# Forgetting attention in a two-layer encoder: another order of the TensorE work inside a step, and one VectorE wait narrowed

## The chip, the cores and the metric

One NeuronCore of a Trainium2 chip runs the whole kernel. The metric is the device time of one execution in microseconds. Three runs of the kernel before gave 1349.3, 1349.78 and 1350.14 us; the median is 1349.78 us.

## What is computed

The kernel computes two layers of an encoder over 512 tokens with 1024 features. Layer 0 mixes a gated recurrence with differential attention; layer 1 is forgetting attention. Each layer ends with an output projection, a layer norm, a SwiGLU block and another layer norm. The change touches the forgetting attention alone:

```python
def _fox_attention(q, k, v, c):          # 16 heads of width 64, 512 tokens
    ...
        s = jnp.einsum('bhqd,bhkd->bhqk', qb, k) * scale + (cb[..., :, None] - c[..., None, :])
        q_pos = start + jnp.arange(Q_BLOCK)
        mask = k_pos[None, :] <= q_pos[:, None]
        p = jax.nn.softmax(jnp.where(mask, s, MASK_VALUE), axis=-1)
        return jnp.einsum('bhqk,bhkd->bhqd', p, v)

def _odd_mixer(x, w_in, w_out, b_f, qn_g, kn_g):
    proj = x @ w_in
    q, k, v, g, f_logit = jnp.split(proj, [D_MODEL, 2 * D_MODEL, 3 * D_MODEL, 4 * D_MODEL], axis=-1)
    ...
    o = _fox_attention(qh, kh, vh, c).reshape(Bsz, S, D_MODEL)
    o = o * jax.nn.sigmoid(g.astype(F32))
    return o.astype(x.dtype) @ w_out
```

The per-row term c_t falls out of the softmax; what is added to the scores is -c_s, and a mask of -1e30 above the diagonal.

## The kernel before, in words

**Weight products.** Every projection is made of three fp32r products (`products`, lines 560 to 563: lines L561, L562, L563 of the profile) that split both operands into a high and a low part. ScalarE makes the high part of the weights (L1328), GpSimd the low part (L1281). A "piece" is a quarter of a 2048-column weight chunk against one tile of tokens: 12 matmuls with 512 moving columns, or 24 with 256.

**The work of the attention.** The 16 heads form 8 pairs, and each pair has 4 blocks of 128 queries: 32 units. Unit u belongs to pair u // 4 and to query block i = u % 4, and has (i + 1) * 128 keys. A unit passes through these stages:

- scores (`pair_scores`, line 1121): for each head of the pair one product of queries and keys (L1132; 64 rows of the array are used, head 0 the lower half, head 1 the upper), one product that adds -c_s (L1137; bf16, 48 rows in the same halves), and one product that adds the mask to the last 128 columns (L1140; bf16, all 128 rows). The mask product closes the bank. The two banks are two of the banks 5, 6 and 7.
- VectorE takes the row maximum (L2047, or L2050 and L2051), ScalarE the exponential and its row sum (L1644, semaphore fexp), VectorE multiplies by the reciprocal (L2058, L2061; semaphore fnorm).
- turn (`turn_pair`, line 1143): TensorE transposes the probabilities (L1148; all 128 rows and columns), head 0 into bank 3, head 1 into bank 4. It first waits for fnorm of its unit and for each bank's last reader.
- ScalarE copies bank 3 out (`prob_copy`, L1572), VectorE copies bank 4 out (L2070).
- values (`pair_values`, line 1152): products of v and the turned probabilities (L1167; 64 columns of the array are used, head 0 the lower half, head 1 the upper) into bank 2. When the four blocks of a pair are done, VectorE copies bank 2 out (L2089, or L2009).

**The order.** A list written at build time, `fox_steps` (lines 391 to 400), interleaves the pieces of the remaining projections (queries and keys "h", values "v", gates "g") with the steps s = 0 to 34. Every engine walks the same list in its own program. An entry is (piece, s) or (piece, None); in some stretches one piece stands between two steps, in others two, and before steps 30 to 33 one piece of the output projection. In an entry TensorE does, in this order: the piece; at some entries the transposes of freshly normed queries and keys (`turn_heads`, L1118), which also go into bank 3 and which ScalarE copies out (L1581); then, with a step s, scores of unit s with their mask, turn of unit s - 2, values of unit s - 3.

ScalarE does, in an entry with step s: copies of the last piece's bank (L1350 and L1600), the copy of turned queries and keys (L1581), rounding of a weight chunk (L1328), then the exponential of unit s, which waits for VectorE's maximum, and behind it the copy of bank 3 of unit s - 2. VectorE does the norm work of queries and keys, then the maximum of unit s, the scaling of unit s - 1, the copy of bank 4 of unit s - 2, and then whatever reads bank 2 (unit s - 3). Pieces take banks 0 and 1 in turn; a piece that begins a new result waits until ScalarE has copied the result before last out of that bank.

The lines that matter in `open_bank` and in the two transposing functions:

```python
                if last[bank]:
                    who, count = last[bank]
                    pe.wait_ge(freed[who][bank], count)
...
                acc = open_bank(key, 3, "act")                                   # turn_heads
...
                    acc = open_bank(("fT", u, m), 3 + m, ("act", "dve")[m])      # turn_pair
```

and the end of a step in ScalarE's program:

```python
                    act.wait_ge(S["fmax"], s + 1)
...
                    act.sem_inc(S["fexp"], 1)
                if s is not None and 2 <= s < F_UNITS + 2:
                    prob_copy(s - 2)
```

Of the kernel before, what the change touches and what calls it, by code (L numbers as in the profile page):

```python
# [39 lines left out]
P = 128  # L40
D = 1024
TS = 512
NT = TS // P
# [22 lines left out]
PAIRS = FH // 2  # L66
# [76 lines left out]
def build(nc, w, out):  # L143
# [5 lines left out]
    with ExitStack() as ctx:  # L149
# [24 lines left out]
        ident_bf = place("ident_bf", [P], BF16, 2)  # L174
        fox_mask = place("fox_mask", [P], BF16, 2)
# [71 lines left out]
        psum = [banks[:, b, :] for b in range(8)]  # L247
# [66 lines left out]
        def chunk_at(stage, i=0):  # L314
            return stage_chunks[stage][i]
# [22 lines left out]
        n = 0  # L338
# [51 lines left out]
        F_UNITS = PAIRS * NT  # L390
# [133 lines left out]
        def _(pe):  # L524
# [13 lines left out]
            def close_bank(key, ins):  # L538
                ins.then_inc(bank_full[uses[key][0]], 1)
# [46 lines left out]
            def token_chunk(c, reader, src_hi, src_lo, k_base, first, final, width=512, places=None):  # L586

                stage, _, size = chunks[c]
                nk = size // width
                if c in by_piece:  # L590
                    pe.wait_ge(hi_ready, c + 1)
                else:
                    weights_in(c)
                for t in range(NT):
                    key = (stage, t) if not isinstance(final, tuple) else (*final, t)
                    if first:
                        open_bank((stage, "acc", t, c), places[t] if places else next_gemm_bank(), reader)
                        acc_bank[t] = uses[(stage, "acc", t, c)]
                    acc = psum[acc_bank[t][0]][:, 0:width]
                    for k in range(nk):  # L600
                        if c in by_piece and t == 0:
                            piece_in(c, k)
                        tok = slice(t * P, (t + 1) * P)
                        ins = products(acc, src_hi[:, k_base + k, tok], src_lo[:, k_base + k, tok],
                                       hi(c, k * width, width), lo(c, k * width, width),
                                       first and k == 0, bool(final) and k == nk - 1)
                    if final:
                        uses[key] = acc_bank[t]
                        close_bank(key, ins)
                    if t == NT - 1:  # L610
                        if final:
                            used_with_bank(c, key)
                        else:
                            used_alone(c, ins)
                    yield
# [505 lines left out]
            def pair_scores(s):  # L1121
                pair, i = s // NT, s % NT
                j, n = s // PART_UNITS, (i + 1) * P
                if s == 0:
                    pe.wait_ge(S["c_in"], 16 * 6)
                if s % PART_UNITS == 0:
                    pe.wait_ge(S["qk_done"], NT * (j + 1))
                    pe.wait_ge(S["v_done"], NT * max(1, j))
                accs = [open_bank(("fs", s, m), SCORE_BANKS[s % 3][m], "act") for m in range(2)]
                for m, acc in enumerate(accs):  # L1130
                    rows = slice(m * HD, (m + 1) * HD)
                    mm(acc[:, 0:n], qk[rows, j % 2, 0, pair % 2, i * P:(i + 1) * P], qk[rows, j % 2, 1, pair % 2, 0:n],  # L1132
                       start=True, stop=False)
                for m, acc in enumerate(accs):
                    h = 2 * pair + m
                    rows = slice(m * HD, m * HD + 3 * FH)
                    mm(acc[:, 0:n], pick[rows, h:h + 1].to_broadcast([3 * FH, P]), c_rows[rows, 0:n],  # L1137
                       start=False, stop=False)
                for m, acc in enumerate(accs):
                    close_bank(("fs", s, m), mm(acc[:, n - P:n], ident_bf[:, :], fox_mask[:, :],  # L1140
                                                start=False, stop=True))

            def turn_pair(u):
                pe.wait_ge(S["fnorm"], u + 1)
                for m in range(2):
                    acc = open_bank(("fT", u, m), 3 + m, ("act", "dve")[m])
                    for j in range(u % NT + 1):
                        ins = nc.tensor.transpose(acc[:, j * P:(j + 1) * P], p_fox[:, u % 3, m, j * P:(j + 1) * P],  # L1148
                                                  ident[:, :])
                    close_bank(("fT", u, m), ins)  # L1150

            def pair_values(u):
                pair, i = u // NT, u % NT
                pe.wait_ge(S["fpT_a"], u + 1)
                pe.wait_ge(S["fpT_b"], u + 1)
                bank = 5 if u == F_UNITS - 1 else 2
                if i == 0 or pair == PAIRS - 1:
                    open_bank(("fv", u), bank, "dve")
                else:

                    bank_count[2] += 1
                    uses[("fv", u)] = (2, bank_count[2], "dve")
                tok = slice(i * P, (i + 1) * P)
                for j in range(i + 1):
                    for m in range(2):
                        h = 2 * pair + m
                        ins = mm(psum[bank][m * HD:(m + 1) * HD, tok], v_all[:, j, h * HD:(h + 1) * HD],  # L1167
                                 pT_fox[:, u % 2, m, j * P:(j + 1) * P], start=j == 0, stop=j == i)
                close_bank(("fv", u), ins)

            first_out[1] = token_chunk(chunk_at("out1"), "dve", o_hi4, o_lo4, 0, True, False, places=(0, 1, 6, 7))
            for i, (piece, s) in enumerate(fox_steps):
                if piece and i >= len(HEAD_LEAD) - 1:
                    stage = chunks[piece[0]][0]
                    if stage not in running:
                        if stage[3] == "h":
                            running[stage] = heads_chunk(int(stage[4]), HEAD_ORDER)
                        elif stage == "foxv0":
                            running[stage] = columns(stage, "act", places=(5, 7, 6, 2))
                        elif stage[3] == "g":  # L1180
                            running[stage] = feature_chunk(piece[0], "act")
                        else:
                            running[stage] = token_chunk(piece[0], "act", xT_hi, xT_lo, 0, True, True, 256)
                    next(running[stage])
                if heads_at(i - TURN_LAG):
                    turn_heads(*heads_at(i - TURN_LAG))
                if s is None:
                    continue
                if F_UNITS - 2 <= s < F_UNITS + 2:
                    if s == F_UNITS - 2:  # L1190
                        for gen in running.values():
                            drain(gen)
                        pe.wait_ge(S["o_hi"], 4)
                        pe.wait_ge(S["o_lo"], 4)
                    next(first_out[1])
                if s < F_UNITS:
                    pair_scores(s)
                if 2 <= s < F_UNITS + 2:
                    turn_pair(s - 2)
                if s >= 3:  # L1200
                    pair_values(s - 3)
            gemm_banks[0] = 4
            fox_out()
            swiglu(1)
# [463 lines left out]
        def _(dve):  # L1668
# [349 lines left out]
            for i, (piece, s) in enumerate(fox_steps):  # L2018
# [53 lines left out]
                if s is not None and s >= 3:  # L2072
                    u = s - 3
                    pair, t = u // NT, u % NT
                    acc = full(("fv", u))
                    if pair == PAIRS - 1:
                        tok = slice(t * P, (t + 1) * P)
                        release(out_gate(pair, acc[:, tok], tok), ("fv", u))
                        dve.sem_inc(S["o_gated"], 1)
                        if t == 0:  # L2080
                            out_lo(4)
                            out_lo(5)
                            out_lo(PAIRS - 2)
                        out_lo(pair, tok, t)
                    elif t == NT - 1 and pair == PAIRS - 2:
                        release(out_gate(pair, acc[:, :]), ("fv", u))
                        dve.sem_inc(S["o_gated"], 1)
                    elif t == NT - 1:
                        release(v.tensor_copy(oT[:, pair, :], acc[:, :]), ("fv", u))  # L2089
# [64 lines left out]
```

## Time and profile before

| | before |
|---|---|
| median of three runs | 1349.78 us |
| the profiled execution | 1350.16 us |
| its span, first to last instruction | 1348.1 us |
| steps 0 to 31, from the first scores to the last values | about 712 to 943 us of the span |
| TensorE matmul (PE) busy | 1334.4 us, 99% |
| TensorE weight load (PEld) busy | 1092.7 us, 81% |
| VectorE (DVE), ScalarE (ACT), GpSimd (POOL) busy | 454.5, 480.0, 529.8 us |

A row of the timeline gives the start of a group of like instructions in us from the start of the span, the time from the first start to the last end, the engine, the line, the operation, what it writes and reads, the shapes and the count. A matmul's own length in it is a latency: the next one starts long before it ends. So the time that a group costs TensorE is read from its start to the start of the next group. Two matmuls of fp32 data stand for one product in L1132 and L1167. A bracket at the end gives idle time of the engine before the group and who ended it.

### The profile page before, as it was taken

To read this page: it belongs to the slowest core of one execution; us is meant where nothing else is said; L and a number is where in the kernel's file an instruction comes from. 1 tells how busy PE (TensorE), PEld (TensorE's weight loads), DVE (VectorE), ACT (ScalarE), POOL (GpSimd) and SP (SyncE) were. 2 spreads that over 40 slices of the span, in tenths; PEclk is the share of its full clock that TensorE was granted. 3 is DMA by queue.
4 is the path that set the end of the run, shared out by engine and by line. 5 is a ranking of instruction groups with operands and counts; after the bars stand their busy time and mean duration, and the time that the engine had idled before them with its cause. 6 is when DMAs were issued, how large, how long until landed. Compare 5 with 4: busy or idle time off the path is not lost.

```text
span 1348.1 us, 17988 instructions
## 1 busy us (share of the span) xinstructions
PE 1334.4 (99%) x6943; PEld 1092.7 (81%) x6943; DVE 454.5 (34%) x857; ACT 480.0 (36%) x759; POOL 529.8 (39%) x421
## 2 busy tenths in 40 slices
PE   9999999999999999999999999999999999999997
PEld 7888877788888888888787877677898888888886
DVE  4364446771111111011643554545621111110105
ACT  3413266533222223211365554644332222222120
POOL 4422433334444444543352332323244444435440
PEclk9999999999999999999999999999999999999999
DMA  6301121314333332323123212313133333333221
GB/s 213 123 32 63 63 94 63 95 38 119 95 94 94 95 101 90 137 94 109 47 84 94 63 33 63 95 63 95 32 110 110 94 94 94 94 109 107 107 84 63
DMA packets 141540, 119.55 MB, mean 89 GB/s; under 512 B 5808, under 2 KB 120720, under 8 KB 141456
## 3 DMA queue, kind: packets, MB, share of 16 engines
q1 hardware_dynamic: 141216, 118.10, 27.9%
q8 instruction: 56, 0.92, 0.3%
q10 hardware_dynamic: 240, 0.31, 0.1%
q14 instruction: 28, 0.23, 0.1%
HBM read 116.20 MB, written 2.10 MB: 88 GB/s over the span
## 4 chain that ended last, share of the span: by engine, by line
PE 96%; DVE 2%; issue 1%; ACT 0%; DMA 0%; POOL 0%; SPq 0%; DVEq 0%; ACTq 0%; POOLq 0%
PE banks L561 28%; PE banks L563 28%; PE banks L562 28%; PE banks L989 2%; PE banks L1132 2%; PE banks L1167 2%; PE banks L1148 1%; PE banks L674 1%; PE banks L1080 1%; PE banks L1007 1%; PE banks L1067 1%; PE banks L1140 1%; PE banks L1118 0%; DMA x_res<-in_x_dram 0%; PE banks L1094 0%
## 5 line engine op out<-in xcount | busy, mean ns | idle before, releaser
L1281 POOL TENSOR_TENSOR w_lo<-w_raw,w_hi 128x512 fp32r<-128x512 f32 x417 | 529.6, 1299 | 786.9 <-ACT w_hi L1328 523.7
L561 PE MATMUL banks<-xT_lo,w_hi 128*128 128x512 f32 (+2 forms) x1024 | 383.7, 375 | 0.9 <-DVEq L1688 0.7
L563 PE MATMUL banks<-xT_hi,w_hi 128*128 128x512 f32 (+2 forms) x1024 | 380.0, 371 | 0.0
L562 PE MATMUL banks<-xT_hi,w_lo 128*128 128x512 f32 (+2 forms) x1024 | 379.9, 371 | 0.0
L1328 ACT ACTIVATE w_hi<-w_raw 128x2048 fp32r<-128x2048 f32 (+1 forms) x106 | 198.2, 1869 | 174.5 <-PE banks L563 145.6
L561 PEld LDWEIGHTS banks<-xT_lo,w_hi 128*128 128x128 f32 (+1 forms) x1024 | 191.4, 187 | 35.7 <-issue 3.3
L563 PEld LDWEIGHTS banks<-xT_hi,w_hi 128*128 128x128 f32 (+1 forms) x1024 | 191.3, 187 | 34.0
L562 PEld LDWEIGHTS banks<-xT_hi,w_lo 128*128 128x128 f32 (+1 forms) x1024 | 191.5, 187 | 32.6
L1960 DVE TENSOR_TENSOR banks<-silu_g,banks 128x512 f32<-128x512 f32 x44 | 30.6, 696 | 402.3 <-PE banks L563 402.3
L561 PE MATMUL banks<-w_lo,xT_hi 128*128 128x512 f32 (+1 forms) x352 | 135.9, 386 | 1.6 <-ACT q_raw L1350 0.7
L561 PE MATMUL banks<-w_lo,hT_hi 128*128 128x512 f32 x352 | 137.1, 390 | 0.0
L563 PE MATMUL banks<-w_hi,hT_hi 128*128 128x512 f32 x352 | 137.0, 389 | 0.0
L562 PE MATMUL banks<-w_hi,hT_lo 128*128 128x512 f32 x352 | 136.9, 389 | 0.0
L1544 ACT ACTIVATE silu_g<-banks 128x512 f32<-128x512 f32 x44 | 26.4, 599 | 306.7 <-PE banks L563 306.6
L563 PE MATMUL banks<-w_hi,xT_hi 128*128 128x512 f32 (+1 forms) x352 | 130.6, 371 | 0.0
L562 PE MATMUL banks<-w_hi,xT_lo 128*128 128x512 f32 (+1 forms) x352 | 130.5, 371 | 0.0
L1892 DVE SCALAR_TENSOR_TENSOR x_res<-x_res,banks 128x512 f32<-128x512 f32 x32 | 22.0, 688 | 204.9 <-PE banks L563 203.8
L561 PEld LDWEIGHTS banks<-w_lo,xT_hi 128*128 128x128 f32 x352 | 66.3, 188 | 16.4 <-issue 4.0
L562 PEld LDWEIGHTS banks<-w_hi,hT_lo 128*128 128x128 f32 x352 | 66.1, 188 | 13.7
L563 PEld LDWEIGHTS banks<-w_hi,hT_hi 128*128 128x128 f32 x352 | 66.1, 188 | 13.7
L561 PEld LDWEIGHTS banks<-w_lo,hT_hi 128*128 128x128 f32 x352 | 66.1, 188 | 13.7
L563 PEld LDWEIGHTS banks<-w_hi,xT_hi 128*128 128x128 f32 x352 | 66.3, 188 | 12.0
(196 smaller groups left out, 1214.6 us busy)
## 6 DMA issues: line engine op xcount, KB each, us to landing
w_raw<-in_ffn_w_dram SPq DMA_DIRECT2D x92, 512.0 KB, 4.4
w_raw<-in_ffn_w_dram SPq DMA_DIRECT2D x20, 1024.0 KB, 4.9
w_raw<-in_even_w_in_dram SPq DMA_DIRECT2D x13, 1024.0 KB, 4.8
w_raw<-in_fox_w_in_dram SPq DMA_DIRECT2D x16, 512.0 KB, 4.4
w_raw<-in_fox_w_in_dram SPq DMA_DIRECT2D x8, 1024.0 KB, 5.6
w_raw<-in_even_w_out_dram SPq DMA_DIRECT2D x4, 1024.0 KB, 4.9
w_raw<-in_fox_w_out_dram SPq DMA_DIRECT2D x4, 1024.0 KB, 4.9
x_res<-in_x_dram SPq DMA_DIRECT2D x4, 512.0 KB, 7.1
```

The source lines that it names most:

```text
L561: mm(acc, l_hi, r_lo, start=first, stop=False)
L562: mm(acc, l_lo, r_hi, start=False, stop=False)
L563: return mm(acc, l_hi, r_hi, start=False, stop=final)
L674: ins = nc.tensor.transpose(acc[:, j * P:(j + 1) * P], src[:, t, f:f + P], ident[:, :])
L989: ins = mm(halves(acc[:, tok], z)[:, :, 1, :], k[:, tok], halves(q[:, tok], z)[:, :, 1, :], start=True, stop=True)
L1132: mm(acc[:, 0:n], qk[rows, j % 2, 0, pair % 2, i * P:(i + 1) * P], qk[rows, j % 2, 1, pair % 2, 0:n], start=True, stop=False)
L1167: ins = mm(psum[bank][m * HD:(m + 1) * HD, tok], v_all[:, j, h * HD:(h + 1) * HD], pT_fox[:, u % 2, m, j * P:(j + 1) * P], start=j == 0, s ...
L1281: ins = nc.gpsimd.tensor_tensor(w_lo[c % RING][:, a:a + n], w_raw[c % RAW][:, a:a + n], w_hi[c % RING][:, a:a + n].bitcast(F32), ALU.subtract)
L1328: chain(fn(w_hi[c % RING][:, 0:size], w_raw[c % RAW][:, 0:size], ACT.Copy), hi_ready)
L1544: release(fn(silu_buf(j), acc[:, :], ACT.Silu), (f"up{l}", j, 0))
L1892: release(stt(xs, xs, ALPHA, full(key)[:, :], ALU.mult, ALU.add), key)
L1960: release(tt(h_buf(j), silu_buf(j), acc[:, :], ALU.mult), (f"up{l}", j, 1))
```

## The change

Inside a step TensorE now does: turn of unit s - 2, scores of unit s without the mask, values, and last the masks of unit s. The values of units s - 4 and s - 3 are done together in every second step (s = 4, 6, ..., 30); steps 31 to 34 do one unit each, as before. VectorE no longer waits in every step for the values of unit s - 3; it waits in the steps in which it reads bank 2. The programs of ScalarE, GpSimd and the queues are as they were, and so is `fox_steps`.

```diff
@@ pair_scores, and the new pair_masks
                        start=False, stop=False)
-                for m, acc in enumerate(accs):
-                    close_bank(("fs", s, m), mm(acc[:, n - P:n], ident_bf[:, :], fox_mask[:, :],
+
+            def pair_masks(s):
+
+                n = (s % NT + 1) * P
+                for m, b in enumerate(SCORE_BANKS[s % 3]):
+                    close_bank(("fs", s, m), mm(psum[b][:, n - P:n], ident_bf[:, :], fox_mask[:, :],
                                                 start=False, stop=True))
@@ after pair_values
+            def values_of(s):
+
+                if s >= F_UNITS - 1:
+                    return [s - 3]
+                return [s - 4, s - 3] if s >= 4 and s % 2 == 0 else []
@@ TensorE's loop over fox_steps
                     next(first_out[1])
+                if 2 <= s < F_UNITS + 2:
+                    turn_pair(s - 2)
                 if s < F_UNITS:
                     pair_scores(s)
-                if 2 <= s < F_UNITS + 2:
-                    turn_pair(s - 2)
-                if s >= 3:
-                    pair_values(s - 3)
+                for u in values_of(s):
+                    pair_values(u)
+                if s < F_UNITS:
+                    pair_masks(s)
@@ VectorE's loop over fox_steps
                     pair, t = u // NT, u % NT
-                    acc = full(("fv", u))
+                    if pair == PAIRS - 1 or t == NT - 1:
+                        acc = full(("fv", u))
                     if pair == PAIRS - 1:
```

## Rows read from the trace of the kernel before

**Rows 1.** The page, busy time of each engine over the span.

```profile
PE 1334.4 (99%) x6943; PEld 1092.7 (81%) x6943; DVE 454.5 (34%) x857; ACT 480.0 (36%) x759; POOL 529.8 (39%) x421
```

**Rows 2.** The page, the chain that ended last, by engine.

```profile
PE 96%; DVE 2%; issue 1%; ACT 0%; DMA 0%; POOL 0%; SPq 0%; DVEq 0%; ACTq 0%; POOLq 0%
```

**Rows 3.** Busy time by stretch: stretch, length, engines, granted clock, DMA share, GB/s.

```profile
712.30:943.50 231.20, 229.28 (x1494) 171.43 (x1493) 120.91 (x257) 125.62 (x273) 65.57 (x52) 1.00 0.23 69
```

**Rows 4.** Timeline of step 9 (256 keys), TensorE, and ScalarE's copy of bank 3.

```profile
771.80 0.39 PE L563 MATMUL banks<-w_hi,xT_hi 128*128 128x512 f32 x1
772.12 0.70 PE L1132 MATMUL banks<-qk 64*128 64x256 f32 x4
772.65 0.28 PE L1137 MATMUL banks<-c_rows,pick 48*128 48x256 bf16 x2
772.86 0.29 PE L1140 MATMUL banks<-fox_mask,ident_bf 128*128 128x128 bf16 x2
772.99 1.04 PE L1148 MATMUL banks<-ident,p_fox 128*128 128x128 f32 x8
...
773.96 0.88 PE L1167 MATMUL banks<-pT_fox,v_all 128*64 128x128 f32 x12
...
774.76 0.50 PE L561 MATMUL banks<-w_lo,xT_hi 128*128 128x512 f32 x1
...
775.11 0.40 PE L562 MATMUL banks<-w_hi,xT_lo 128*128 128x512 f32 x1
...
775.41 0.60 ACT L1572 ACTIVATE pT_fox<-banks 128x512 f32<-128x512 f32 x1 [0.17 <-ACT p_fox L1644]
```

**Rows 5.** Timeline of step 0 (128 keys), TensorE: masks with a piece right behind.

```profile
712.30 0.49 PE L1132 MATMUL banks<-qk 64*128 64x128 f32 x4
712.62 0.22 PE L1137 MATMUL banks<-c_rows,pick 48*128 48x128 bf16 x2
712.78 0.29 PE L1140 MATMUL banks<-fox_mask,ident_bf 128*128 128x128 bf16 x2
712.87 0.48 PE L561 MATMUL banks<-w_lo,xT_hi 128*128 128x512 f32 x1
713.19 0.39 PE L562 MATMUL banks<-w_hi,xT_lo 128*128 128x512 f32 x1
```

**Rows 6.** Timeline around step 11 (512 keys), TensorE, VectorE and ScalarE.

```profile
785.66 0.39 PE L563 MATMUL banks<-w_hi,xT_hi 128*128 128x512 f32 x1
...
785.89 0.60 PE L1118 MATMUL banks<-ident,qn 128*128 128x128 f32 x4
786.42 1.13 PE L1132 MATMUL banks<-qk 64*128 64x512 f32 x4
...
786.59 0.98 ACT L1581 ACTIVATE qk<-banks,gains 128x256 f32<-128x256 f32 x2 [1.52 <-PE banks L1118]
...
787.70 0.29 PE L1140 MATMUL banks<-fox_mask,ident_bf 128*128 128x128 bf16 x2
...
788.14 1.22 DVE L2047 TENSOR_REDUCE small<-banks 128x2 f32<-128x1024 f32 x1 [1.67 <-PE banks L1140]
788.36 0.44 PE L1167 MATMUL banks<-pT_fox,v_all 128*64 128x128 f32 x4
788.73 0.50 PE L561 MATMUL banks<-w_lo,xT_hi 128*128 128x512 f32 x1
...
791.16 0.39 ACT L1572 ACTIVATE pT_fox<-banks 128x256 f32<-128x256 f32 x1 [0.17 <-ACT p_fox L1644]
```

**Rows 7.** Timeline after step 19: bank 3 copied out, then its next user.

```profile
849.74 0.38 ACT L1572 ACTIVATE pT_fox<-banks 128x256 f32<-128x256 f32 x1 [0.17 <-ACT p_fox L1644]
850.27 0.63 PE L1118 MATMUL banks<-ident,qn 128*128 128x128 f32 x4
850.29 0.60 ACT L1350 ACTIVATE q_raw<-banks 128x512 f32<-128x512 f32 x1 [0.17 <-ACT pT_fox L1572]
```

**Rows 8.** Timeline before step 3: the only piece that waits for its bank.

```profile
727.34 0.50 PE L561 MATMUL banks<-w_lo,xT_hi 128*128 128x512 f32 x1 [0.73 <-ACT q_raw L1350]
```

## The prediction, made before the changed kernel was run

> **What bounds the kernel now.** I read the page first: TensorE is busy 99% of the span [rows 1], and the chain that ended last runs through it for 96% [rows 2]. Then the stretch of the change: from the first scores to the last values it takes 231.2 us, TensorE is busy for 229.3 of them at a granted clock of 1.00, which is the 2.4 GHz level, while VectorE and ScalarE are at about half [rows 3]. So a microsecond taken from TensorE's order is a microsecond of the kernel, and every microsecond that TensorE is made to wait is one too. The timeline of a step then says what the order costs beyond the matmuls themselves, and how long after the masks the other engines need for their part; these two decide.
>
> **Part 1, fewer changes of the array's shape.** A step before goes through four changes: piece (all of the array) to scores (row halves), to masks and turn (all), to values (column halves), to the next piece (all). Their prices, group start to group start:
> - Into the scores: 771.80 to 772.12 is 0.32, where the next matmul of a piece or a transpose comes after 0.23, 785.66 to 785.89 [rows 4, 6]: 0.09. The scores take 0.32 at 128 columns [rows 5] and 0.53 at 256 [rows 4]: 0.21 for each 128, so 0.11 is not columns. Together 0.20.
> - Out of them, into the masks: the c products take 0.16 and 0.21 [rows 5, 4], 0.05 for each 128, so 0.11 is the change. Two masks cost 0.13 before a turn, 0.02 above two matmuls of 0.055 each.
> - Turn into values: eight transposes take 0.97 [rows 4], four 0.53 before the scores [rows 6]: 0.11 each, 0.09 left, in front of the row halves and in front of the column halves alike.
> - Values to the next piece: twelve take 0.80 [rows 4], four 0.37 [rows 6]: 0.054 each, 0.155 left; and the piece's second matmul comes after 0.35 instead of 0.23. Together 0.27, of which some 0.05 belongs to entering the values.
>
> A step before: 0.09 + 0.11 + 0.11 + 0.02 + 0.09 + 0.155 + 0.12, some 0.69. New in front of a piece are the masks: 712.78 to 713.19 is 0.41 for two masks and one matmul (0.34), so 0.07 [rows 5]. A piece followed by transposes costs nothing, the 0.23 above [rows 6]. A new step without values is then 0.09 + 0.11 + 0.11 + 0.07 = 0.38, a gain of 0.31; there are 14 (s = 3, 5, ..., 29). A new step with values adds scores to values, which no row shows. Its bounds are 0 (column halves prepared beside row halves) and the dearest change seen, 0.27; I take 0.14, what entering the values costs from the transposes, the nearest row. It adds values to masks at 0.11, the price of c to masks: 0.63, a gain of 0.06, between -0.07 and 0.20; there are 15 (s = 4, ..., 30, and 31). Steps 0, 1 and 32 to 34 keep their changes, step 2 loses 0.05. Rounded down for the hundredths in the rows, 14 x 0.30 + 15 x 0.05 = **4.9 us gained**, with 3 and 7 as bounds. Doing values in pairs moves no matmul away and adds none.
>
> The Trainium skill, "TensorEngine Tiling (Array Packing)", section "Key Properties", says that changing the tiling mode drains the engine while changing the tile does not. The trace agrees that changes cost 0.13 to 0.27. Counted by that rule alone, 128 changes become 85; 43 at a mean of 0.17 would be 7.3 us.
>
> **Part 2, the masks come last and the turn first.** No instruction is added, but the order meets two single banks. The mask closes the scores' bank, and behind it stand, each in its engine's order: VectorE's maximum, ScalarE's two exponentials of unit s, and only then ScalarE's copy of bank 3 of unit s - 2 (VectorE's scaling of unit s - 1 and its copy of bank 4 follow the same maximum). The next turn, of unit s - 1, needs all of these. Before, it had a turn, values, a piece and scores to cover that; now it has the pieces between two steps and nothing else.
>
> How long is the chain? Step 11: masks start at 787.70, the maximum at 788.14, ScalarE's copy ends at 791.55; TensorE restarts 0.15 after such a copy, 850.12 to 850.27, where a transposing group waits for bank 3 already now [rows 7]: 4.00 after the masks [rows 6]. Step 9, with 256 keys: 776.01 + 0.15 - 772.86 = 3.30 [rows 4]. The cover with one piece is 0.13 for the masks, 0.05 of change and 12 x 0.233 = 2.80: 2.97. So the turn waits 1.03 after a step with 512 keys and 0.33 after one with 256. With two pieces the cover is 5.8 and nothing waits.
> - One piece and nothing else follows steps 3, 7, 11, 15, 23 (512 keys), 5, 9, 13 (256), 20 (128) and 30 (384): 5 x 1.05 + 3 x 0.4 + 0.4 + 0.5 = **7.4 us**. The value for 384 keys lies between the two measured; the one for 128 I raise, since a scaling of 512 columns is in VectorE's chain.
> - Transposed queries and keys (L1118) sit in the same bank 3. Six times (before steps 3, 7, 11, 15, 22, 23) they stand directly before the step, so directly before the turn. Today ScalarE empties the bank beside the scores: 786.59 to 787.57 [rows 6]. The turn could start at 785.89 + 4 x 0.11 = 786.33 and would wait until 787.57 + 0.15: 1.39, and 1.35 as I take it. **6 x 1.35 = 8.1 us.**
> - Where the transposes of queries and keys follow the first piece after a step (8 times: after steps 4, 6, 12, 14, 18, 19, 21, 22), they find bank 3 with unit s - 2 still in it: arrival 2.97, ready at 3.2 to 4.2 after the masks. Waits of 0.3 to 0.5, near 1 after step 19 and 0.7 after step 22: **4.1 us.**
> - A second piece that opens the bank whose last result ScalarE copies only behind the copy of bank 3: the first such wait is there now [rows 8]. After step 10 the result comes 0.17 + 0.60 after the copy [rows 7], about 4.2 after the masks, for an arrival at 2.97: 1.25 us. After steps 4, 12 and 19 it is some 0.2, after step 2 0.1: **2.0 us.**
> - The end: after step 31 (512 keys) the pattern of step 11 once more. Some wait stands there already; I add **0.7 us.**
>
> Together 22.3 us of waits. Each is too short to be absorbed: TensorE is the bound before and behind it. What queues behind a waiting turn is all of the step and the next piece. Bounds: the waits computed with step 9's chain everywhere and without the bank cases give 10; each 0.2 longer, since scaling and GpSimd's subtraction meet at other times, gives 27.
>
> **Part 3, VectorE's wait.** VectorE reads bank 2 only at the end of a pair and in the last pair. Without the narrower wait it would sit for values that come a step later. With it there is nothing: the values stand before the masks, and VectorE comes to them after the maximum. Price 0; in the steps that keep it, the copies of bank 2 and the gates hide it.
>
> Other movements that cost nothing: GpSimd's low parts wait for normed queries, which come up to 2 us later against the pieces; the weights made in one such round are used several us later. The DMA queues are moved past nothing.
>
> **Sum.** The profiled execution took 1350.16 us. 1350.16 - 4.9 + 22.3 = 1367.6; the median of the runs lies 0.4 below that execution, so 1367.
>
> **The rivals.**
> - Only the clear bank conflict bites: the six turns directly behind queries and keys (8.1 us), while the chains after the masks get shorter as VectorE and ScalarE have cleared their other work by then. For it: in a few steps VectorE was late for the maximum because of other work. Against it: in step 11 it started 0.44 after the masks began, with idle time before it [rows 6], so there is nothing left to shorten. 1350.2 - 4.9 + 8.1, about 1353.
> - Faster: the changes of shape decide. Place: the seams of all 29 steps; price 0.30 and 0.05 a step. It decides if the waits stay under 4.9 us in all, that is under 0.2 us a gap: 1345, if ScalarE's copy of bank 3 were done before the next turn. The rows speak against it: one piece is 2.97 and the shortest of the chains above is 3.3. By the skill's rule alone, with every change at one price, it would be 1342.5.
> - Waits lower the clock: in the dense part (steps 18 to 23) TensorE would be idle more often than anywhere now, and at 1.2 GHz a matmul with 512 columns takes twice its 0.233. Ten microseconds of that level cost 5 to 10 us more: 1375. The rows show the clock at 1.00 through idle times of 0.7 [rows 3, 8]; longer ones they don't show.
> - The change does what it says; there is no rival in which it doesn't, since every piece of it is in TensorE's own program.
>
> **How the numbers follow.** Forecast 1367 with a chance of 0.80; only the bank conflict 0.08; faster 0.07; the clock 0.05. A measurement of this kernel can tell about 0.2%, 2.7 us. The forecast's own bounds are 1355 and 1372; the middle of them, with the rest on the upper side for the clock, gives 1358 to 1373, leaving out the faster case, the case of 1353 and a slice above. Faster by over 0.2%: 0.07. Within: 0.03, the lower half of the case of 1353 (which ends at 1352.5). Slower: 0.90.
>
> **What would show it.** In the changed profile: steps without values 0.3 us shorter from piece to piece, apart from waits; L1148 with idle time before it ended by ScalarE's L1581 six times at about 1.3 us, and by L1572 or L2070 after the single-piece steps at 0.3 to 1.1; L1118 waiting for L1572; L561 waiting for L1350 after step 10. TensorE's busy time about the same or less, its idle time 20 us more in 712 to 960 us. It would be wrong if TensorE showed no idle time in front of L1148, or if ScalarE's copy of bank 3 ended less than 2.8 us after the masks.

## The result, and the profile after

The changed kernel takes 1366.97 us (four runs, 1366.42 to 1367.96), the kernel before 1349.74 us beside it. The ratio is 1.0128, with a 95% interval of 1.0115 to 1.0141: **1.3% slower**. The forecast was 1367.

The page of the changed kernel, busy time by engine and the chain that ended last:

```profile
PE 1331.4 (98%) x6943; PEld 1093.7 (80%) x6943; DVE 455.2 (33%) x857; ACT 480.0 (35%) x759; POOL 529.6 (39%) x421
...
PE 91%; DVE 3%; ACT 2%; issue 2%; DMA 0%; POOL 0%; DVEq 0%; ACTq 0%; SPq 0%; POOLq 0%
```

TensorE is busy 3.0 us less than before [rows 1], and yet the kernel is longer. The chain that ended last was TensorE's for 96% and VectorE's for 2% [rows 2]; now TensorE has 91% of it, and VectorE and ScalarE have 5% together. The stretch from the first scores to the last values, which was 231.20 us with TensorE busy for 229.28 [rows 3], is in the changed kernel (columns: stretch, its length, busy time of PE, PEld, DVE, ACT, POOL, granted clock, DMA share, GB/s):

```profile
712.10:959.55 247.45, 227.19 (x1493) 172.55 (x1492) 120.83 (x257) 125.39 (x273) 65.55 (x52) 1.00 0.22 65
```

It is 16.25 us longer by these two windows, 16.5 if both are taken to the end of the last value matmul (943.52 and 959.78), and the two profiled executions differ by 16.26 (1366.42 against 1350.16). So all of it is here. Two microseconds less of busy time and 18.3 us more of idle time make it up. Who ends TensorE's idle time, from the list of waits of the changed kernel in this part (idle time in us, times, longest; L1152 is the turn, L1118 the transposes of queries and keys, L1593 ScalarE's copy of the latter, L1584 its copy of bank 3, L1362 its copy of a piece's bank; L1171 is the values):

```profile
PE banks L1152 <- ACT qk L1593: 7.1, 6, 1.2
PE banks L1152 <- ACT pT_fox L1584: 6.5, 9, 1.1
PE banks L1118 <- ACT pT_fox L1584: 3.4, 7, 1.1
PE banks L561 <- ACT q_raw L1362: 2.1, 2, 1.2
PE banks L1171 <- ACTq L1585: 0.6, 1, 0.6
```

The kernel before had, of all these, one wait of L561 [rows 8], the last line, and 0.2 us before a turn at the end. The two kinds of wait can be followed in the timeline of the changed kernel around step 11 (start, length, engine, line, what, idle time before and who ended it):

```profile
792.35 0.60 PE L1118 MATMUL banks<-ident,qn 128*128 128x128 f32 x4
...
793.05 0.98 ACT L1593 ACTIVATE qk<-banks,gains 128x256 f32<-128x256 f32 x2 [1.51 <-PE banks L1118]
794.17 0.63 PE L1152 MATMUL banks<-ident,p_fox 128*128 128x128 f32 x4 [1.22 <-ACT qk L1593]
794.73 1.13 PE L1132 MATMUL banks<-qk 64*128 64x512 f32 x4
...
796.01 0.29 PE L1144 MATMUL banks<-fox_mask,ident_bf 128*128 128x128 bf16 x2
...
796.44 1.23 DVE L2059 TENSOR_REDUCE small<-banks 128x2 f32<-128x1024 f32 x1 [3.52 <-PE banks L1144]
...
797.70 0.69 ACT L1656 ACTIVATE p_fox<-banks,small 128x512 f32<-128x512 f32 x1 [3.67 <-DVE small L2059]
...
799.46 0.38 ACT L1584 ACTIVATE pT_fox<-banks 128x256 f32<-128x256 f32 x1 [0.17 <-ACT p_fox L1656]
799.99 0.85 PE L1152 MATMUL banks<-ident,p_fox 128*128 128x128 f32 x6 [0.89 <-ACT pT_fox L1584]
```

The same work stood in [rows 6]. There the scores followed L1118 and covered ScalarE's copy. Now the turn follows it and wants the same bank: four transposes of 0.11 end at 792.79, the turn starts at 794.17, so 1.38 us are lost. Below, the masks start at 796.01 and the next turn at 799.99, 3.98 us later, where the piece between them is done after 2.94 (its last matmul starts at 798.72, and the next instruction could follow 0.23 later).

The seams of a step with values, step 8 of the changed kernel:

```profile
770.27 0.49 PE L1132 MATMUL banks<-qk 64*128 64x128 f32 x4
770.60 0.22 PE L1137 MATMUL banks<-c_rows,pick 48*128 48x128 bf16 x2
770.75 0.88 PE L1171 MATMUL banks<-pT_fox,v_all 128*64 128x128 f32 x12
771.56 0.29 PE L1144 MATMUL banks<-fox_mask,ident_bf 128*128 128x128 bf16 x2
771.66 0.48 PE L561 MATMUL banks<-w_lo,xT_hi 128*128 128x512 f32 x1
```

From the c products to the values it takes 0.15, as from them to the masks in [rows 5], 0.16: 0.05 of it is columns, so 0.10 is the change. Entering the values from the transposes costs 0.09 at the same place [rows 4]. Twelve value matmuls take 0.81 before the masks, 0.80 before a piece in [rows 4]. So the seam that no row showed, from row halves to column halves, costs what entering the values from the transposes costs.

### The profile page after: what moved, and what is told of

It reads as the page before. It is cut to its first block, busy times and chain, and to the rows that moved or that the text cites. A ratio compares the mean times of both kernels' runs of the same rounds, so it can differ in the third digit from the quotient of the medians.

```text
span 1364.3 us, 17967 instructions
## 1 busy us (share of the span) xinstructions
PE 1331.4 (98%) x6943; PEld 1093.7 (80%) x6943; DVE 455.2 (33%) x857; ACT 480.0 (35%) x759; POOL 529.6 (39%) x421
## 4 chain that ended last, share of the span: by engine, by line
PE 91%; DVE 3%; ACT 2%; issue 2%; DMA 0%; POOL 0%; DVEq 0%; ACTq 0%; SPq 0%; POOLq 0%
PE banks L561 27%; PE banks L563 26%; PE banks L562 26%; PE banks L989 2%; PE banks L1132 2%; PE banks L1152 1%; PE banks L1171 1%; ACT p_fox L1656 1%; PE banks L674 1%; DVE small L2059 1%; PE banks L1080 1%; PE banks L1007 1%; PE banks L1067 1%; ACT pT_fox L1584 1%; PE banks L1144 1%
## 5 line engine op out<-in xcount | busy, mean ns | idle before, releaser
L561 PE MATMUL banks<-xT_lo,w_hi 128*128 128x512 f32 (+2 forms) x1024 | 383.4, 374 | 0.9 <-DVEq L1700 0.7
L561 PEld LDWEIGHTS banks<-xT_lo,w_hi 128*128 128x128 f32 (+1 forms) x1024 | 191.5, 187 | 34.0 <-issue 1.5
L561 PE MATMUL banks<-w_lo,xT_hi 128*128 128x512 f32 (+1 forms) x352 | 135.5, 385 | 3.1 <-ACT q_raw L1362 2.1
L561 PE MATMUL banks<-w_lo,hT_hi 128*128 128x512 f32 x352 | 137.1, 390 | 0.0
L561 PEld LDWEIGHTS banks<-w_lo,xT_hi 128*128 128x128 f32 x352 | 66.4, 189 | 15.5 <-ACT q_raw L1362 2.9
L561 PEld LDWEIGHTS banks<-w_lo,hT_hi 128*128 128x128 f32 x352 | 66.1, 188 | 13.7
```

What stands on the lines that cost most here:

```text
L561: mm(acc, l_hi, r_lo, start=first, stop=False)
```

## The experiments

All are edits of TensorE's loop over the steps, of one engine's order beside it, or of the bank that L1118 writes. A time with a ratio and its interval is the median of six to eleven executions; the other times are of one execution each. The kernel before took 1349.9 us beside them.

**1. Values in pairs alone**, on the kernel before, with VectorE's narrower wait that this needs. Scores, masks and turn keep their order.

```diff
-                if s >= 3:
-                    pair_values(s - 3)
+                for u in values_of(s):
+                    pair_values(u)
```

> The kernel before, with one part of the change: values of two units every second step (and VectorE's narrower wait that this needs); scores, masks, turn keep their order. Theory (changes of the array's shape are worth what the seams say, and the waits of the changed kernel come from the turn standing first and the masks last): 14 steps lose turn-to-values and values-to-piece, 0.34 us each, 4.8 us; the cover of the copies keeps the scores, so no new wait but some 0.3 us more in front of L1118 after step 19. 1345.5 us, ratio 0.9967. Rival (doing values late and in pairs is itself what makes TensorE wait, since the buffers of turned probabilities come free later): waits in front of L1148 and L1167, and a time above 1352.

1345.91 us, ratio 0.9969 (0.9956 to 0.9981): **0.3% faster than the kernel before**. Two of the waits that are left:

```profile
PE banks L1118 <- ACT pT_fox L1578: 0.8, 1, 0.8
PE banks L561 <- ACT q_raw L1356: 0.8, 1, 0.8
```

Pairing the values is the good part of the change. It costs little waiting: its whole list adds up to 2.8 us, that of the kernel before to 1.5.

**2. The turn behind the scores again**, values and masks last, on the changed kernel.

```diff
-                if 2 <= s < F_UNITS + 2:
-                    turn_pair(s - 2)
                 if s < F_UNITS:
                     pair_scores(s)
+                if 2 <= s < F_UNITS + 2:
+                    turn_pair(s - 2)
```

> The changed kernel with the turn put back behind the scores; values and masks stay last. Theory (the turn is early: its cover is the pieces alone): every wait of a turn shrinks by the scores in front of it, 0.6 us for 128 keys to 1.25 for 512; directly behind L1118 from 8.1 to about 1 us in all, after steps of 512 keys from 1.1 to 0.5 each, after steps of 256 keys to nothing; the waits of L1118 (4.3) and L561 (2.4) stay. Some 12 us less than the changed kernel: 1354. Rival (the masks at the end alone make the chain late, wherever the turn stands): it stays within 3 us of 1366.

1356.78 us, 10.2 us below the changed kernel (theory 12, rival at most 3). The list of waits of this kernel:

```profile
PE banks L1118 <- ACT pT_fox L1584: 3.4, 7, 1.1
PE banks L561 <- ACT q_raw L1362: 2.1, 2, 1.2
PE banks L1152 <- ACT pT_fox L1584: 1.6, 4, 0.4
...
PE banks L1152 <- ACT qk L1593: 0.2, 1, 0.2
```

The waits of the turn behind L1593 fall from 7.1 to 0.2 us and those behind L1584 from 6.5 to 1.6, while the first two lines are what they were, to the tenth. The estimate was 2.8 us too low, and not because of the waits: counted from start to start they fall by 12.3 us, as the theory had it, while the two profiled executions differ by 9.6. The other 2.7 us go to the array's shape, which the estimate left out. In this order a step with values goes from row halves to the whole array for the turn, then to column halves, then back for the masks, one change more than in the changed kernel, in 15 steps.

**3. The masks behind the scores again**, turn first, on the changed kernel.

```diff
                 if s < F_UNITS:
                     pair_scores(s)
+                    pair_masks(s)
                 for u in values_of(s):
                     pair_values(u)
-                if s < F_UNITS:
-                    pair_masks(s)
```

> The changed kernel with the masks put back directly behind the scores, ahead of the values; the turn stays first. Theory: in steps without values nothing changes, so the waits after odd steps and the six directly behind L1118 stay (some 17 us); those after even steps (after 4, 6, 10, 12, 14, 18, 20, 22, 30), 4.7 us, go, because 0.7 to 1.5 us of values come between masks and piece; 14 steps pay 0.15 us more for the array's shapes, 2.1. About 1364. Rival (the masks' lateness is the whole cause): 1350 to 1352.

1362.26 us, 4.7 below the changed kernel. Its waits:

```profile
PE banks L1152 <- ACT qk L1592: 7.1, 6, 1.2
PE banks L1152 <- ACT pT_fox L1583: 5.1, 7, 1.1
PE banks L1118 <- ACT pT_fox L1583: 1.3, 2, 1.1
```

Only the waits after steps with values shrink, since only there did the masks move; the rival is out. The time is 1.7 us under the estimate: the waits, counted from start to start, fell by 5.3 and not 4.7, and the changes of shape cost 1.4 more and not 2.1; the rest is the difference between single executions.

Experiments 1, 2 and 3 and the changed kernel form a square, since all four have the values in pairs. With the masks and the turn in their old places the time is 1345.91; with the masks last alone it is 10.9 us more, with the turn first alone 16.4 more, with both 21.1 more. So the two costs do not add up. The 10.2 and 4.7 us of these two experiments are what each move costs beside the other; either of them alone would already have made the kernel slower than before.

**4. All copies first**, on the changed kernel: ScalarE's copy of bank 3 ahead of its exponentials, and VectorE's scaling and copy of bank 4 ahead of its maximum.

```diff
+                if s is not None and 2 <= s < F_UNITS + 2:
+                    prob_copy(s - 2)
                 if s is not None and s < F_UNITS:
                     n = (s % NT + 1) * P
                     act.wait_ge(S["fmax"], s + 1)
...
                     act.sem_inc(S["fexp"], 1)
-                if s is not None and 2 <= s < F_UNITS + 2:
-                    prob_copy(s - 2)
```

(and in VectorE's loop the block of the maximum moved behind those of the scaling and of the copy)

> TensorE's order as in the changed kernel; ScalarE's copy of bank 3 stands ahead of its exponentials, and VectorE's scaling and copy of bank 4 stand ahead of its maximum, so none of them waits for the masks of its step. Theory: the waits of turns behind a single piece (8.4 us) and of L1118 (4.3) go, L561 behind ScalarE's q_raw copy shrinks from 2.4 to about 1.3; the six turns directly behind L1118 keep their 8.1 us, since they wait for another user of bank 3. About 1353. Rival (the softmax chain itself, not the place of the copies in the engines' order, is too long for the cover): waits in front of L1152 ended by VectorE's scaling instead, and a time above 1360.

1362.01 us. The time is where the rival put it, above 1360 and not at 1353, but waits of the kind that it named, ended by VectorE's scaling, make up only 0.7 us. The largest waits of this kernel:

```profile
PE banks L1152 <- ACT qk L1593: 9.1, 6, 3.1
PE banks L561 <- ACT q_raw L1362: 3.4, 3, 1.9
PE banks L1132 <- ACT p_fox L1658: 1.8, 2, 1.3
```

The waits for the copy of bank 3 are gone, and others have come. The timeline of the longest of them, from the masks of step 21 on:

```profile
868.42 0.28 PE L1144 MATMUL banks<-fox_mask,ident_bf 128*128 128x128 bf16 x2
868.50 2.48 DVE L2058 TENSOR_SCALAR p_fox<-p_fox,small 128x128 f32<-128x128 f32 x2
...
871.95 0.69 DVE L2078 TENSOR_REDUCE small<-banks 128x2 f32<-128x512 f32 x1 [0.24 <-DVE pT_fox L2067]
...
873.96 0.98 ACT L1593 ACTIVATE qk<-banks,gains 128x256 f32<-128x256 f32 x2
...
875.08 0.41 PE L1152 MATMUL banks<-ident,p_fox 128*128 128x128 f32 x2 [3.12 <-ACT qk L1593]
```

VectorE's maximum starts 3.5 us after the masks instead of 0.4, because scaling and copy stand in front of it; ScalarE's exponentials, and the copy of turned queries and keys behind them, are late by as much. Part of the time is also TensorE's clock (last section). Two things had been moved at once, and the second hid the first. Experiment 5 moves one.

**5. ScalarE's copy first, alone**: the ScalarE part of experiment 4, VectorE as in the changed kernel.

> The changed kernel with one move alone: ScalarE's copy of bank 3 ahead of its exponentials. VectorE keeps its order, with the maximum first. Theory (the copies-first run added waits because VectorE's maximum came 2 us later, not because the copy was no cause): in front of turns behind a single piece 8.4 us become about 1.5, ended by VectorE's copy or scaling now; the waits of L1118 (4.3) go; L561 behind q_raw 2.4 to about 1; the six turns directly behind L1118 keep 8.1. 1354.5. Rival (the length of the softmax chain is the cause, in whatever order the copies stand): over 5 us stay in front of single-piece turns and the time is above 1358.

1354.01 us. Its waits:

```profile
PE banks L1152 <- ACT qk L1593: 7.1, 6, 1.2
PE banks L561 <- ACT q_raw L1362: 2.1, 3, 0.8
PE banks L1152 <- DVE p_fox L2073: 1.1, 2, 0.9
```

The lines with L1584, 6.5 and 3.4 us in the changed kernel, are gone. The cause of those waits is the place of one copy in ScalarE's order, not the length of the softmax. The six turns behind L1118 wait as before.

**6. L1118 in a bank of its own**, on the changed kernel: the score bank that the next step leaves free.

```diff
-                acc = open_bank(key, 3, "act")
+                nxt = next(s for _, s in fox_steps[i:] if s is not None)
+                acc = open_bank(key, 7 - nxt % 3 if nxt else 3, "act")
```

> The changed kernel with the transposes of queries and keys (L1118) in the score bank that the next step leaves free, instead of bank 3. Theory (six turns wait because L1118 sits in their bank): the 8.1 us in front of turns directly behind L1118 go; of the 4.3 us in front of L1118 about 1 stays, now ended by ScalarE's exponential; the waits behind a single piece stay at 8 to 8.5. 1355. Rival (those turns wait for the chain of their own unit, whatever bank L1118 uses): six waits of 0.3 to 1.3 us before the same steps stay, ended by L1584 or VectorE's scaling, and the time is above 1361.

1357.23 us. Its two largest waits:

```profile
PE banks L1153 <- ACT pT_fox L1585: 7.1, 10, 1.1
PE banks L561 <- ACT q_raw L1363: 4.0, 4, 1.5
```

No turn waits for the copy of queries and keys any more, and nothing waits in front of L1118. But 1.9 us of what L1118 no longer waits for turn up one instruction later, in front of the piece whose bank ScalarE has yet to copy: the 2.2 us by which the estimate was too low.

**7. Both causes away**: experiments 5 and 6 in one kernel, TensorE's order as in the changed kernel.

> The same, and L1118 in the score bank that the next step leaves free: both causes of waits taken away, the changed kernel's order in TensorE kept. Theory (22 us of waits against 5 us of shape changes saved is all there is to the change): the gain shows, 1347, ratio 0.998. Rival (something else in the changed order costs time, such as the seam from row halves to column halves): above 1350.

1346.72 us, ratio 0.9977 (0.9968 to 0.9986). What waits:

```profile
PE banks L561 <- ACT q_raw L1363: 2.1, 3, 0.8
PE banks L1153 <- DVE p_fox L2074: 0.9, 1, 0.9
```

The account closes: with these waits removed, the order of the change is 3.1 us faster than the kernel before. Its whole list of waits still adds up to 4.0 us against 1.5 there, so the changes of shape give back about 5.6 us, and the seam from row halves to column halves holds no surprise.

**8. VectorE's narrower wait alone**, on the kernel before.

> The kernel before with VectorE's narrower wait alone. Theory: VectorE was never late for anything through that wait, ratio 1.000, within 0.1%. Rival (VectorE was held there, and its scaling comes earlier now): some tenths of a us less in front of the turns of the last steps, 0.9995.

1349.77 us, ratio 0.9999 (0.9990 to 1.0008): no difference.

**9. Another order from the same prices: turn last.** Scores, values in pairs, masks, turn: one change of shape fewer in a step with values than in the kernel before, and the turn keeps the scores as cover.

```diff
-                if 2 <= s < F_UNITS + 2:
-                    turn_pair(s - 2)
                 if s < F_UNITS:
                     pair_scores(s)
                 for u in values_of(s):
                     pair_values(u)
                 if s < F_UNITS:
                     pair_masks(s)
+                if 2 <= s < F_UNITS + 2:
+                    turn_pair(s - 2)
```

> A new order from the prices found: scores, values of two units in every second step, masks, turn last. Row halves, column halves, all of the array: 0.19 + 0.14 + 0.11 in a step with values and 0.30 in one without, against 0.65 in each step of the kernel before, 8 us less; the turn's cover is its own unit's turn before it, the piece and the scores. Theory: no turn waits; L1118 and L561 in steps after 384 keys wait a few tenths each and 1 us once, since only two transposes stand in front, some 3.5 us over the kernel before. 1345.5, ratio 0.997. Rival (values ahead of the masks make the chain late enough to stall turns again): waits in front of the turn over 4 us and a time above 1349.

1349.24 us, ratio 0.9995 (0.9986 to 1.0004): no difference from the kernel before, and a miss of 3.7 us. Two of its waits, and granted clock (the last but two of the columns) in three stretches near its end:

```profile
PE banks L1171 <- DVE oT L2021: 2.3, 1, 2.3
PE banks L1118 <- ACT pT_fox L1584: 1.9, 3, 1.0
```

```profile
932.00:935.70 3.70, 2.36 (x15) 2.06 (x16) 3.20 (x7) 1.01 (x3) 1.35 (x2) 0.69 0.90 275
935.70:937.20 1.50, 1.50 (x6) 1.23 (x6) 1.36 (x5) 0.13 (x1) 0.00 (x0) 0.62 0.89 259
937.20:940.00 2.80, 2.80 (x22) 2.02 (x21) 1.02 (x3) 0.31 (x1) 0.00 (x0) 1.00 0.87 256
```

No turn waits, as expected, so the rival is not the reason, though the time is as high as it had said; the loss is at the end. In the last steps the values now stand in front of the turn and want copies that VectorE makes late. Behind the 2.3 us of idle time TensorE was at its lower level, 1.2 GHz: the granted clock is 0.54 from 933.3 to 937.0 (the stretches above mix in idle time before and full clock after).

**10. Turn last, L1118 in its own bank.**

> The same order, and L1118 in the score bank that the next step leaves free. Theory: the waits in front of L1118 go as well, 2 us; 1343.5, ratio 0.9955, faster than values in pairs alone (1345.9). Rival (bank 3 is no cost in this order): the same time as with the turn last alone, within 0.5 us.

1347.25 us, ratio 0.9982 (0.9973 to 0.9991), 2.0 us less than experiment 9 and again 3.7 above the estimate. The 2 us look like the gain that was expected of the own bank, but the traces say otherwise. The lists of waits add up to 6.9 us in experiment 9 and to 6.8 here: what L1118 no longer waits for stands in front of other instructions. The idle time of 2.34 us at the end is there as well. What differs is the clock behind it, which stayed at 1.00 here; that alone is 1.6 us (last section). Whether it falls in every execution of experiment 9 is not shown.

**11. The same with the end mended**: from step 31 on scores, masks, turn, values.

> Scores, values, masks, turn, with L1118 in the free score bank, and the last steps (from step 31) with scores, masks, turn, values. Theory (the turn-last order lost 3.5 us at the end, where values in front of the turn wait for copies that only just began): these waits shrink to 1.8, 1344.5, faster than values in pairs alone. Rival (the 2.7 us are needed anyway, since VectorE's work at the end sets them): 1347.

1345.56 us, ratio 0.9969 (0.9958 to 0.9981). The end gains 1.7 us of the 2.8 expected; a new wait takes the rest:

```profile
PE banks L1153 <- DVE p_fox L2077: 1.3, 1, 1.3
```

**12. Values in pairs, L1118 in its own bank**, on the kernel before.

> Values in pairs alone, and L1118 in the free score bank. Theory: of the 0.9 + 0.3 us around L1118 after step 19 about 0.8 goes, nothing comes: 1345.1. Rival: the wait only moves to L561 behind q_raw, as 1.2 us did in the turn-last order: 1345.9.

1345.91 us, ratio 0.9971 (0.9960 to 0.9982), the time of experiment 1: the rival was right, and in this order too the own bank is worth nothing. The wait moved, from L1118 to the piece behind it:

```profile
847.69 0.47 PE L561 MATMUL banks<-xT_lo,w_hi 128*128 128x512 f32 x1 [1.08 <-ACT q_raw L1357]
```

Experiments 1, 11 and 12 are the fastest versions found and their intervals do not tell them apart (1345.9, 1345.6 and 1345.9); the first is the smallest edit.

## Why the prediction was right

I counted all waits from start to start in the two traces, less what the instruction in front needs, over the stretch of the change. That sum is 24.6 us in the changed kernel and 2.9 in the kernel before: 21.8 us more, where the forecast had 22.3. The stretch grew by 16.3, so the changes of shape gave back 5.5, where it had 4.9. The 5.5 is a remainder of this count, which holds to about half a microsecond; experiment 7 comes to about 5.6. The two errors, half a microsecond each, have the same sign in the sum and leave 1 us; that the median met the forecast within 0.1 us is partly luck, since the median lies 0.5 above the profiled execution here and 0.4 below it in the kernel before.

- **Changes of shape: right in the sum, by some luck, with one price wrong.** The seam that no row showed was taken at 0.14 by the nearest row, and the rows of step 8 bear it out. But the 0.63 for a step with values counts 0.11 too much: it keeps the change from the c products to the masks, where the values now stand between them. The same prices give 0.20 into the scores, 0.14 into the values, 0.11 out of them and 0.07 in front of the piece, 0.52 in all. Such a step gains 0.17 and not 0.06, and the sum would have been about 6.5 us, 1 us above the count. That microsecond is open, and it is more than the 0.6 by which the wrong sum missed. The sentence that changes cost 0.13 to 0.27 does not fit the list before it either, which has 0.09 to 0.27. Experiment 1 gains 4.0 us where 14 steps at 0.34 were expected to bring 4.8, less the 0.3 that it loses in front of L1118.
- **Six turns behind L1118: right.** Forecast 8.1, counted 8.1 from start to start, 1.33 or 1.39 each. Experiments 2, 5 and 6 tell the cause from every other: it goes with a cover or with another bank, and stays when the other copy moves.
- **Turns behind a single piece: right.** The forecast was 7.4 us and 0.7 at the end, on top of 0.6 that stood there; counted, 8.4 for all. The chain of step 11, forecast at 4.00 us from masks to turn, measures 3.98. Experiment 5 shows that it is ScalarE's copy behind the exponentials that makes it so long.
- **L1118 behind the first piece: right.** Forecast 4.1, counted 4.0 (4.3 less 0.3 from before), at seven places instead of eight. The two long ones, forecast near 1 and at 0.7, are 1.3 each.
- **A piece behind its bank: right.** Forecast 2.0, counted 1.8.
- **VectorE's wait: right**, by experiment 8.
- **The rival that the clock falls** did not happen in the changed kernel: the clock in the stretch is 1.00, as in [rows 3], with idle times up to 1.2 us. It did happen in experiments 4 and 9, after longer ones (last section). There a matmul with 512 columns took 0.43 from start to start, and not quite twice 0.233.
- **The rule on drains.** The Trainium skill, "TensorEngine Tiling (Array Packing)", section "Key Properties", has a change of tiling mode drain the engine and a change of tile not. The traces agree as far as time shows it: entering the values costs 0.10 in step 8, while the products of the two heads, on the two halves, start 0.007 us apart. Counted with one price for each change the rule would have promised 7.3 us; the count gives 5.5. The price depends on the pair: c products to masks is 0.11, values to a piece up to 0.27.

The rival on the other side, a gain, was sound in its first half: the order does save 5.5 us. It failed where the forecast put it, at a cover of 2.97 us against a chain of 3.3 to 4.2.

## What to carry to other kernels

Before an instruction is moved forward on a full engine, write down each buffer that it reuses, who empties it, and what stands in front of that reader in its own engine's order; the time between the instruction's new place and the event that starts that chain is all the cover there is. Split such a change into its parts and time each: here one part (values in pairs) was worth 4 us, and the order of the rest cost 21. When a single buffer is relieved, look one instruction further, since the same late engine often holds the next buffer too.

## What the runs showed of the hardware

The clock of TensorE stayed at its upper level (2.4 GHz, granted 1.00 in the row above) through the 25 idle times of up to 1.2 us of the changed kernel's list of waits. So it did in experiment 6 through one of 1.5 us. Four in the kept traces of this stretch are longer, and three of them were followed by the lower level, 1.2 GHz:

- In experiment 4 TensorE was idle for 1.9 us before 728.13; the clock was still 1.00 until 729 and 0.50 from 730 to 732. The stretch from 728.2 to 732.3, with 0.67 as its mean:

```profile
728.20:732.30 4.10, 4.10 (x13) 3.15 (x14) 2.54 (x7) 1.05 (x3) 0.65 (x1) 0.67 0.00 0
```

- In the same execution, after the idle time of 3.1 us that ends at 875.08, it was 0.50 from 877 to 879.
- In experiment 9, after 2.34 us, it was about 0.5 from 933.5 to 936.5. From the start of the values to the fourth matmul of the next piece it took 3.57 us there (933.34 to 936.91).
- In experiment 10, after the same 2.34 us at the same place, it stayed at 1.00, and the same work took 2.00 us (931.82 to 933.82), 1.6 less:

```profile
931.82 0.66 PE L1172 MATMUL banks<-pT_fox,v_all 128*64 128x128 f32 x8 [2.34 <-DVE oT L2022]
```

```profile
931.80:935.70 3.90, 3.88 (x26) 3.22 (x26) 3.64 (x8) 0.80 (x2) 0.03 (x1) 1.00 0.92 276
```

So a wait that grows past what this kernel had before can cost more than its own length, but the length of the idle time alone does not settle it. What else does is not shown here.

The price of a change between the array's shapes depends on the pair. Into the values it is the same from row halves (0.10, step 8 above) and from the whole array (0.09 [rows 4]), while a piece behind fp32 values loses up to 0.27 [rows 4]. Not every such loss is a change of shape: a piece behind the bf16 masks loses 0.07 [rows 5], and both use the whole array.
